# Two transformer-like blocks on one core: the opening loads x by column halves and takes the first weight unit in four slices

## The reference

```python
h = rms_norm(x, pre_mix_norm[l])     # x * rsqrt(mean(x^2)) * gain
proj = h @ w_in[l]                   # 1024 channels in, all projections of the mixer
```

## Time and profile before

| what | value |
|---|---|
| median of three runs | 932.22 us (930.96 to 933.86) |
| the profiled execution, its own time | 934.1 us |
| its span, first to last instruction | 932.3 us |
| mean granted TensorE clock | 0.980 |
| TensorE products busy | 875.4 us (94%) |
| VectorE, ScalarE, GpSimd busy | 596.2, 463.9, 78.4 us |
| HBM traffic | 143.83 MB, 154 GB/s on the mean |
| chain that ended last | PE 81%, DVE 9%, ACT 4%, DMA 1% |

### The profile page before, as it was taken

How to read it: one execution, slowest core, us unless ns; L and a number is a source line. 1 busy time by engine, 2 the same in 40 slices (tenths; PEclk the granted TensorE clock), 3 DMA queues, 4 the chain that set the end, 5 groups by cost and what they waited for, 6 DMA issues and landing times.

```text
span 932.3 us, 15563 instructions
## 1 busy us (share of the span) xinstructions
PE 875.4 (94%) x6246; PEld 809.9 (87%) x6246; DVE 596.2 (64%) x765; ACT 463.9 (50%) x648; POOL 78.4 (8%) x78
## 2 busy tenths in 40 slices
PE   3999897999999999889999999889998899999997
PEld 3999797999988899789999999779985799999995
DVE  4348756535777578669676776766645576556654
ACT  5356763236856534457455555464444454433332
POOL 0025661100000032000000000000000000000000
PEclk9999898999999999999999999999998999999999
DMA  8442333142433435626555456253321435555541
GB/s 321 170 181 91 136 136 136 54 149 104 143 136 130 153 141 181 226 95 233 181 181 192 173 185 217 91 181 136 103 79 68 180 133 207 181 185 190 196 150 46
DMA packets 21736, 143.83 MB, mean 154 GB/s; under 512 B 3008, under 2 KB 3012, under 8 KB 5168
## 3 DMA queue, kind: packets, MB, share of 16 engines
q1 hardware_dynamic: 19872, 138.30, 41.5%
q0 software_dynamic: 1808, 4.73, 1.5%
HBM read 141.96 MB, written 1.84 MB: 154 GB/s over the span
## 4 chain that ended last, share of the span: by engine, by line
PE 81%; DVE 9%; ACT 4%; issue 3%; DMA 1%; POOL 1%; SPq 0%; ACTq 0%; DVEq 0%; POOLq 0%
PE pj L467 16%; PE pj L469 13%; PE pj L470 13%; PE pa L862 6%; PE pa L863 6%; PE pa L864 6%; DVE area L1555 3%; PE pj L471 2%; DVE w_lo L1542 2%; PE pj L472 2%; PE pa L506 2%; PE pj L562 1%; PE pj L563 1%; PE pj L564 1%; DVE area L1558 1%
## 5 line engine op out<-in xcount | busy, mean ns | idle before, releaser
L467 PE MATMUL pj<-a_hi,w_hi 128*128 128x256 f32 x1184 | 340.3, 287 | 12.0 <-DVE w_lo L1542 9.1
L1542 DVE TENSOR_TENSOR w_lo<-w_raw,w_hi 128x2048 fp32r<-128x2048 f32 x128 | 300.1, 2347 | 76.9 <-ACT w_hi L1101 76.9
L469 PE MATMUL pj<-a_lo,w_hi 128*128 128x256 f32 x1184 | 337.0, 285 | 0.0
L470 PE MATMUL pj<-a_hi,w_lo 128*128 128x256 f32 x1184 | 336.8, 284 | 0.0
L1101 ACT ACTIVATE w_hi<-w_raw 128x2048 fp32r<-128x2048 f32 x128 | 243.8, 1906 | 74.1 <-PE pa L864 43.3
L467 PEld LDWEIGHTS pj<-a_hi,w_hi 128*128 128x128 f32 x1184 | 229.2, 194 | 17.0 <-issue 16.0
L469 PEld LDWEIGHTS pj<-a_lo,w_hi 128*128 128x128 f32 x1184 | 229.3, 194 | 0.9
L470 PEld LDWEIGHTS pj<-a_hi,w_lo 128*128 128x128 f32 x1184 | 229.1, 193 | 0.0
L862 PE MATMUL pa<-w_hi,a_hi 128*128 128x512 f32 x280 | 110.2, 394 | 1.8 <-issue 1.8
L863 PE MATMUL pa<-w_lo,a_hi 128*128 128x512 f32 x280 | 110.0, 393 | 0.0
L864 PE MATMUL pa<-w_hi,a_lo 128*128 128x512 f32 x280 | 109.7, 392 | 0.0
(11 more groups left out here) (247 smaller groups left out, 1069.2 us busy)
## 6 DMA issues: line engine op xcount, KB each, us to landing
w_raw<-stream SPq DMA_DIRECT2D x128, 1024.0 KB, 4.8
area<-gains POOLq DMA_DIRECT2D x4, 512.0 KB, 3.9
cst<-consts SPq DMA_DIRECT2D x1, 1093.0 KB, 14.0
x_tok<-x_in SPq DMA_DIRECT2D x2, 512.0 KB, 4.6
area<-cmpw POOLq DMA_DIRECT2D x1, 1024.0 KB, 5.5
out<-x_tok SPq DMA_DIRECT2D x4, 256.0 KB, 2.0
t_wide<-t_rows POOLq DMA_DIRECT2D x1, 768.0 KB, 13.3
prm<-params SPq DMA_DIRECT2D x1, 562.5 KB, 10.3
```

What stands on the lines that cost most here:

```text
L467: pe.matmul(out_, a[0], a[1], start=first, stop=False)
L469: pe.matmul(out_, wh, al, start=False, stop=False)
L470: return pe.matmul(out_, wl, ah, start=False, stop=last)
L1542: dve.tensor_tensor(w_lo[:, slot, :], w_raw[:, slot, :], w_hi[:, slot, :].bitcast(F32), ALU.subtract)\
```

## The change

x is no longer loaded by token blocks but by column halves: one load brings columns 0 to 511 of all 256 tokens, another columns 512 to 1023. Unit 0 comes in four loads of 512 columns (two chunks each), each with a semaphore of its own; the last one uses `w_loaded0`. The gains and slice 0 now stand ahead of the second x half, slices 1 to 3 behind it. Bytes are the same.

TensorE turns x by pairs of chunks, q = 0 to 3, both token blocks together, so each bank of `pa` is full after four transposes. A new semaphore `x_first` tells of banks 0 and 2, S and T (of two banks each) of banks 1 and 3. ScalarE and VectorE take bank q (two chunks) and then slice q of the weights, four times over. TensorE runs unit 0 with the chunk outermost and both groups of 128 output columns inside, so it wants slice q only at chunk 2q. The 48 products are the same ones; both halves of the bank accumulate side by side, as `first_pair` does elsewhere. Units 1 and up are as before.

```diff
--- before.py
+++ after.py
@@ -326,11 +326,19 @@
             def first_load(u):
                 sp.dma_start(w_raw[:, u, :], stream[u]).then_inc(S(f"w_loaded{u}"), 16)
 
-            sp.dma_start(x_tok[:, 0, :], x_rows[:, 0, :]).then_inc(S("x_loaded0"), 16)
+            def first_piece(i):
+
+                cols = slice(i * 512, (i + 1) * 512)
+                sp.dma_start(w_raw[:, 0, cols], stream[0][:, cols])\
+                  .then_inc(S(f"w_piece{i}" if i < 3 else "w_loaded0"), 16)
+
+            sp.dma_start(x_tok[:, :, 0:512], x_rows[:, :, 0:512]).then_inc(S("x_loaded0"), 16)
             sp.dma_start(cst[:, 0:o_c], consts[:, 0:o_c]).then_inc(S("base_loaded"), 16)
-            sp.dma_start(x_tok[:, 1, :], x_rows[:, 1, :]).then_inc(S("x_loaded1"), 16)
             sp.dma_start(prm[:, 0:o_g], params[:, 0:o_g]).then_inc(S("gains_loaded"), 16)
-            first_load(0)
+            first_piece(0)
+            sp.dma_start(x_tok[:, :, 512:1024], x_rows[:, :, 512:1024]).then_inc(S("x_loaded1"), 16)
+            for i in range(1, 4):
+                first_piece(i)
             first_load(1)
             sp.dma_start(prm[:, o_g:PW], params[:, o_g:PW]).then_inc(S("prm_loaded"), 16)
             first_load(2)
@@ -567,14 +575,16 @@
 
             pe.wait_ge(S("base_loaded"), 16)
             claim(pe, "S", "x")
-            for tb in range(2):
-                pe.wait_ge(S(f"x_loaded{tb}"), 16)
-                for k in range(KC):
-                    o = (k % 2) * T + tb * P
-                    mm = transpose((ps, pt)[k // 4][:, (k // 2) % 2, o:o + P], x_tok[:, tb, k * P:(k + 1) * P])
-                    if tb == 1 and k == 3:
-                        written(mm, "S")
-            written(mm, "T")
+            for q in range(4):
+                pe.wait_ge(S(f"x_loaded{q // 2}"), 16)
+                for k in (2 * q, 2 * q + 1):
+                    for tb in range(2):
+                        o = (k % 2) * T + tb * P
+                        mm = transpose(pa[:, q, o:o + P], x_tok[:, tb, k * P:(k + 1) * P])
+                if q % 2:
+                    written(mm, "ST"[q // 2])
+                else:
+                    mm.then_inc(S("x_first"), 1)
 
             def scores(q, kT_, o, kpart=slice(0, P)):
 
@@ -636,7 +646,23 @@
                 written(mm, "O")
 
 
-            run_unit(("sbq", 0), operand_gate(0))
+            for k in range(KC):
+                if k % 2 == 0:
+                    if k < 6:
+                        pe.wait_ge(S("piece_hi"), k // 2 + 1)
+                        pe.wait_ge(S("piece_lo"), k // 2 + 1)
+                    else:
+                        unit_ready(0)
+                pe.wait_ge(S("opnd_lo"), k + 1)
+                for nb in range(2):
+                    c = k * 256 + nb * P
+                    o_ = pj[0][:, nb * T:(nb + 1) * T]
+                    pe.matmul(o_, w_hi[:, 0, c:c + P], a_hi[:, k, :], start=(k == 0 and nb == 0), stop=False,
+                              skip_group_check=True)
+                    pe.matmul(o_, w_hi[:, 0, c:c + P], a_lo[:, k, :], start=False, stop=False, skip_group_check=True)
+                    mm = pe.matmul(o_, w_lo[:, 0, c:c + P], a_hi[:, k, :], start=False, stop=(k == KC - 1),
+                                   skip_group_check=True)
+            mm.then_inc(S("unit_done"), 1)
             run_unit(("sbq", 1))
             spread(0)
             for n in (("sbk", 0), ("sbk", 1), ("sbv", 0), ("sbv", 1), ("xbc", 0)):
@@ -1123,11 +1149,8 @@
             def operand(j, gname):
 
                 g = prm_(gname)
-                for k in range(2 if j else 0, KC):
-                    if j:
-                        act.wait_ge(S("x_turned"), 4 * (j - 1) + k // 2 + 1)
-                    elif k % 4 == 0:
-                        await_psum(act, "ST"[k // 4], "x")
+                for k in range(2, KC):
+                    act.wait_ge(S("x_turned"), 4 * (j - 1) + k // 2 + 1)
                     act.activation(a_hi[:, k, :], pa[:, k // 2, (k % 2) * T:(k % 2 + 1) * T], ACT.Copy,
                                    scale=g[:, k:k + 1]).then_inc(S("opnd_hi"), 1)
 
@@ -1164,9 +1187,19 @@
             act.wait_ge(S("eps_ready"), 1)
             warm_root()
             act.wait_ge(S("gains_loaded"), 16)
-            split(0)
-            ahead_of[0] = 1
-            operand(0, "g_mix1")
+            g = prm_("g_mix1")
+            for q in range(4):
+                if q % 2:
+                    await_psum(act, "ST"[q // 2], "x")
+                else:
+                    act.wait_ge(S("x_first"), q // 2 + 1)
+                for k in (2 * q, 2 * q + 1):
+                    act.activation(a_hi[:, k, :], pa[:, q, (k % 2) * T:(k % 2 + 1) * T], ACT.Copy, scale=g[:, k:k + 1])\
+                       .then_inc(S("opnd_hi"), 1)
+                cols = slice(q * 512, (q + 1) * 512)
+                act.wait_ge(S(f"w_piece{q}" if q < 3 else "w_loaded0"), 16)
+                act.activation(w_hi[:, 0, cols], w_raw[:, 0, cols], ACT.Copy)\
+                   .then_inc(S("piece_hi" if q < 3 else "w_hi_done"), 1)
             split(1)
             ahead_of[0] = 2
             x_squares(0, junk_x)
@@ -1638,11 +1671,15 @@
 
             dve.memset(eps_t, EPS).then_inc(S("eps_ready"), 1)
             dve.wait_ge(S("gains_loaded"), 16)
-            for k in range(KC):
-                operand_lo(0, "g_mix1", k)
+            for q in range(4):
+                for k in (2 * q, 2 * q + 1):
+                    operand_lo(0, "g_mix1", k)
+                cols = slice(q * 512, (q + 1) * 512)
+                dve.wait_ge(S("piece_hi" if q < 3 else "w_hi_done"), q + 1 if q < 3 else 1)
+                dve.tensor_tensor(w_lo[:, 0, cols], w_raw[:, 0, cols], w_hi[:, 0, cols].bitcast(F32), ALU.subtract)\
+                   .then_inc(S("piece_lo" if q < 3 else "w_lo_done"), 1)
             read(dve.memset(hid, 0.0), "S")
             read(dve.memset(hid_t, 0.0), "T")
-            split(0)
             split(1)
             ahead_of[0] = 2
             x_spread(0, lambda: ahead(0))
```

## The result

| | before | changed |
|---|---|---|
| median of 17 runs each | 933.29 us | 928.70 us |
| lowest to highest | 930.96 to 934.69 | 924.02 to 931.97 |
| ratio, 95% interval | | 0.9942 (0.9926 to 0.9958) |
| profiled execution | 934.1 us | 931.04 us |
| its span | 932.3 us | 929.2 us |

(One more number belongs to the before column: one of its runs took 2165.67 us and stands in neither the range nor the ratio.) The change gains 4.6 us; the prediction had 8.3, and 928.7 is above its range of 921.3 to 927.3. (The mean of before's other 16 runs is 933.0.)

A forecast was written before the change was run, and what follows sets the result against it. It took the serial opening, ending on unit 0's last low part, as the bound within a chain 81% TensorE. First product 18.53 to 10.2 gives -8.3, extra ScalarE/VectorE work 0, clock 0: from 932.2 to 923.9 us, range 921.3 to 927.3.

The forecast's parts named there:

- its section on ScalarE and VectorE: Opening: slice splits 0.63 us, low parts 0.69; 0.6 us more on ScalarE and 0.5 on VectorE, neither on the path.
- Clock: 0: Term of the sum: the clock adds or takes nothing; 24 slow products kept as before.
- what the opening gives should be kept to the end, one for one: Whole kernel: nothing on the chain waits for a load after the opening, so its 8.3 us reach the end.
- the clock stays low: Rival: stalls between slices keep TensorE at 1.2 GHz beyond unit 0, 0.093 us per product; 89 more eat 8.3. Chance 2%.
- upper bound of 9.0: Landing of the second x half in us, if all bytes after 4.5 us crawl at 221 GB/s.
- The line of landings: Opening loads: before's landing times read at the new order's byte sums; second x half 8.1, taken as 8.2.
- The spare of 1.1 us before unit 1: Opening's end: unit 1's low part ready at 17.1, wanted at 18.2; the thinnest cover, each us beyond costs one.
- all three signs: Forecast wrong if x half 1 lands after 9, products pause before a slice or unit 1, or its low part ends after 18.2.
- a rival at 8%: Opening products: the clock rises sooner; half of 2.2 us back gives 922.8, all of it 921.7. Chance 8%.
- Each further DMA costs in series: Rival, opening loads: 1.35 us per further DMA, first product 12.9, unit 1 at 16.9; gain 5.6, time 926.6. Chance 6%.
- A later load takes the gain back: Rival, behind the opening: a full queue lets unit 2 or 3 set the pace; 931 to 933 us. Chance 4%.

The follow-up runs named there:

- without slices: The change with unit 0 in one load, split whole behind the operand's parts; x halves, pair turning and chunk order kept: 929.58 us, ratio 0.9960 to before.
- later by 3: The change plus 3 products that nobody reads ahead of the spread of the root (1.3 us of work): 927.65 us, ratio 0.9943 to before.
- later by 6: The change plus 6 products that nobody reads ahead of the spread of the root (2.6 us of work), run twice: 927.89 and 927.76 us.
- second and fourth profile of the change: The change unchanged, run again beside the kernel before in two later groups: 925.86 us (ratio 0.9899) and 926.06 us (ratio 0.9913).
- the other three groups: Follow-up groups in which the unchanged change was timed again against the kernel before: 925.86, 927.69 and 926.06 us.
- filled: Products that nobody reads added in five TensorE waits: kernel before 925.65 us, change 918.92, change with x before slice 0 919.26.
- first and third profile of the change: The change unchanged: the profile beside the 17 runs (928.70 us) and that of a later repeat (927.69 us, ratio 0.9923).

## Why the prediction was wrong

**Right: the serial opening made parallel.** The slices are ready before they are wanted, cost 0.63 us (split) and 0.69 us (low part) each, and hide under TensorE, as its section on ScalarE and VectorE said. The first product is released by TensorE's own transposes. The mark at the root moved by 7.6 us in the first profile and by 8.0, 8.6 and 8.0 in the three others of the change; 8.3 was forecast. That the sum of the opening comes so near is partly luck, since two errors in it cancel (below).

**The step that failed: "Clock: 0", and with it "what the opening gives should be kept to the end, one for one".** I took the rest of the program to run as in the profile of before, moved forward. It holds for the waits. It does not hold for the granted clock: in the profiled execution 4.5 of 7.6 us were given back, 4.1 of them in low stretches at 239, 413 and 587 us that before did not have or had shorter. Where a profile has its low stretches at before's places of the program (the one near 710 us at times half as long), the shift is kept to 900 us: 3.9 us of 3.9 without slices, 7.6 of 7.3 in later by 3, 6.9 of 6.6 in later by 6. The second and fourth profile of the change, with other places and the same total, kept 6.5 of 8.0. The same over all runs: span times mean clock, the span at full clock, averages 913.4 us over the 68 runs of before and 906.0 over the 35 of the change, so 7.4 us less, close to the opening's gain; the mean clock is 0.9798 against 0.9788, which at some 930 us is 0.9 us given back. Both figures are rough, since some runs of before count the low clock of the opening and some do not. In the 17 runs of the result the mean clock was 0.9779, nearly another us lost, and those runs gave 4.6; the other three groups gave 8.0, 5.8 and 7.5, each on another chip. Whether the chip has a part in it was not tested; the 17 runs alone span 924.0 to 932.0. Over the runs of the change the time follows the clock (correlation -0.91): 923.5 us at 0.983, 932.0 at 0.976, with the same program. In the kernel before it follows less closely (-0.49). The pooled gain is 6.7 us, or 927.4 for the change (6.5 us if the 16 runs of before in the result are counted too). The forecast of 923.9 assumed the clock of before and no spread from this source; the rival "the clock stays low" looked for the loss in the opening, where there was none, and not 200 us behind it.

**Mis-sized: the landings.** The second x half was taken at 8.2 with an upper bound of 9.0 and landed at 10.0, 9.6, 9.1 and 9.6. Slice 0 at 6.3 came at 8.7 and between 7.7 and 8.3 in the others. Unit 1 at 12.9 came at 14.5, and 13.6 to 14.1. The line of landings was laid over the sums of bytes, as if each load were complete before the next one moved; but by 10.0 us 2.56 MB had been moved, and x was only then complete, with 1.59 MB up to it in the queue. With slice 0 ahead, x lands at 8.2 to 10.0 (ten profiles, 9.1 on the mean); where x is ahead, at 6.8 to 7.8 (four, 7.4). That is 1.7 us for 256 KB, which take 0.7 us at 369 GB/s. Unit 1 scatters as much, from 12.7 to 14.5 in the ten. The upper bound of 9.0 does not come out of its own rate either: the 0.80 MB behind the constants take 3.6 us at 221 GB/s, which gives 8.3. The spare of 1.1 us before unit 1 fell with this, and the gap of 0.48 us at 18.91 is its price; all three signs that the prediction named for being wrong came (x after 9, a pause before unit 1, its low part at 18.76 and not by 18.2). It was hidden in the sum by an error the other way, the clock rising after 8 slow products and not 24 (+1.5 us), which I had as a rival at 8%: the Trainium skill ("TensorE: Matmul & The Clock Gate", section What's actually happening) says that the number of slow products at the start varies from run to run of one kernel, and says not to fit to a count. The trace agrees: 8, 12, 10 and 12 slow products in the four profiles of the change, the spacing changing at 13.4, 13.8, 12.9 and 13.9 us; I had fitted to 24. The rival's argument against itself, that sixteen transposes did not raise the clock, was read from one profile: in two other profiles with before's opening they did, at 8.4 and 9.0 us, and the clock fell again before the products.

**The rivals.** *Each further DMA costs in series*: unit 1 did land later than forecast, but at 12.7 to 14.5 in ten profiles with the changed loads, and at 13.03 with the same number of DMAs and x ahead, and not at 16.9, so the count is not the price. That the order is the price is shown for x only. *A later load takes the gain back*: units 2 and 3 landed at 18.3 and 23.4, and TensorE waited for neither. Why the DMA engines are busy and slow between 4 and 8 us stays open; the runs with other rows of x and another number of loads show no effect of either.

**Does it matter where x stands?** In the profiles the version with x ahead spreads the root 1.5 us sooner than the change's first profile and 0.5 to 1.1 sooner than the others, but its times (medians of 927.17, and 919.26 filled) are those of the change (927.09 over 35 runs, and 918.92 filled). A difference of 1 us is below what 5 runs can tell at this scatter.

The fastest versions run are the change with the waits filled and, level with it, the same with x ahead: 918.92 us, 1.7% below before (1.4 to 2.0%).

## What to carry to other kernels

A gain near the start of a long kernel is an offset of everything behind it. Before it is put down one for one, read the granted clock over the whole span, list its low stretches and the TensorE waits ahead of them, and take into the range what they can add or take away (here 0.8 us per 0.001 of mean clock); for gains under 1%, compare span times mean clock beside the times, if it is recorded alike in both kernels, and look at the runs one by one: they can fall into two sets. Where TensorE waits a few us for another engine and is needed at full clock afterwards, products that nobody reads can be worth as much as a scheduling change (here 6.9 and 8.2 us, beside 4.6 to 8.0), if they are sized from a measured duration. And in the queue of this opening what is awaited first should go first: a load of 256 KB ahead of x cost x 1.7 us.

## What the runs showed of the hardware

- Low stretches of TensorE's clock inside the program lasted 3.4 or 6.8 us each, at 0.50 (1.2 GHz); 3.4 us more of it cost 1.1 to 1.5 us. The wait of 1.75 us was followed by one in the first and third profile of the change, and not in the second and fourth.
- One program, four profiles, 35 runs: 923.5 to 932.0 us, with the time following the clock (correlation -0.91). The kernel before: 68 runs, 57 within 931.0 to 935.4 and 11 within 937.9 to 938.9.
- Sixteen transposes behind one another raised TensorE's clock in two profiles of before's opening (at 8.4 and 9.0 us) and not in a third; it fell again at 11.8 and 12.4 us, while TensorE waited until 18.2 and 18.4.
- A 256-column product of plain float32 took 0.43 us at full clock and left two records; one of the rounded operands takes 0.12 (three of those make one product of float32 accuracy, 0.36).
- In the profile of the change the 16 DMA engines were busy 76 to 101% of the time between 4.5 and 8 us and moved 206 to 303 GB/s; from 9 to 14 us 409 to 463. A load of 512 KB was complete when about 1 MB of later loads had been moved too.
